# A 480-column matmul into two accumulators in the linear layers of a hybrid decoder step

## What is computed

```python
for layer in range(DEPTH):                       # DEPTH = 2
    xp, xs = rms_norm(hp, nw[0]), rms_norm(hs, nw[0])
    # layer 0: nsa(x @ w_in) @ w_out             w_in: 1024 x 2608, w_out: 1024 x 1024
    # layer 1: hgrn(x @ w_in) * gate @ w_out     w_in: 1024 x 4096, w_out: 1024 x 1024
    ...
    h = h + rms_norm(mixer_out, nw[1])
    a, g = split(rms_norm(h, nw[2]) @ w_gu)      # 1024 x 5632
    h = h + rms_norm((silu(a) * g) @ w_down, nw[3])   # 2816 x 1024
```

## Time and profile before

| | |
|---|---|
| time, three runs | 1673.37, 1675.85, 1679.09 us; median 1675.85 |
| profiled execution | span 1673.2 us from its first to its last instruction; no time of its own is listed beside it |
| PE busy | 1589.8 us, 95% of the span, 15534 matmuls and as many weight loads |
| DVE, ACT, POOL busy | 810.0, 554.3, 565.5 us |
| mean granted TensorE clock | 0.969 of full speed |
| largest groups | the six products of L1025, 6720 matmuls of 128x260 |

### The profile page before, as it was taken

The page is one execution under the profiler, slowest core; times in us unless marked ns, Lnnn a source line. Parts: engine busy times, 40 slices in busy tenths (PEclk is TensorE's granted clock), DMA queues, the critical chain, the costliest instruction groups (busy, mean ns, idle before and its releaser), DMA issues. The chain is left out here.

```text
span 1673.2 us, 38351 instructions
## 1 busy us (share of the span) xinstructions
PE 1589.8 (95%) x15534; PEld 1484.1 (89%) x15534; DVE 810.0 (48%) x1353; ACT 554.3 (33%) x1051; POOL 565.5 (34%) x505
## 2 busy tenths in 40 slices
PE   7997898999899999999998999999899999999996
PEld 7997885666599999999998899999799999999995
DVE  4331126566548344443148677675448343443145
ACT  4120115556455222222245433324255222222242
POOL 0002105677524534433016234332014443433013
PEclk9999888999999999999999999999899999999998
DMA  6855988877340222223343334333140222323342
GB/s 208 315 178 180 323 308 337 285 254 257 137 176 20 96 88 88 94 98 105 104 157 113 96 89 149 102 118 87 64 139 27 88 88 89 99 92 104 105 156 86
DMA packets 87375, 238.35 MB, mean 142 GB/s; under 512 B 18333, under 2 KB 21071, under 8 KB 85793
## 3 DMA queue, kind: packets, MB, share of 16 engines
q1 hardware_dynamic: 81528, 221.41, 39.1%
q0 software_dynamic: 3392, 11.02, 1.8%
q10 hardware_dynamic: 2314, 3.96, 0.7%
HBM read 217.81 MB, written 23.77 MB: 144 GB/s over the span
## 5 line engine op out<-in xcount | busy, mean ns | idle before, releaser
L867 DVE TENSOR_TENSOR layer_w_lo<-ring,layer_w_hi 128x1024 fp32r<-128x1024 f32 (+1 forms) x136 | 223.1, 1641 | 258.4 <-ACT layer_w_hi L746 258.4
L1025 PE MATMUL layer_ps<-layer_x_hi,layer_w_hi 128*128 128x260 f32 x1312 | 268.5, 284 | 3.8 <-DVE layer_w_lo L867 2.7
L1025 PE MATMUL layer_ps<-layer_x_hi,layer_w_lo 128*128 128x260 f32 x1312 | 267.8, 284 | 0.0
L1025 PE MATMUL layer_ps<-layer_x_lo,layer_w_hi 128*128 128x260 f32 x1312 | 267.3, 283 | 0.0
L746 ACT ACTIVATE layer_w_hi<-ring 128x1024 fp32r<-128x1024 f32 (+1 forms) x136 | 158.7, 1169 | 206.8 <-PE layer_ps L1025 206.8
L1025 PE MATMUL layer_ps<-layer_h_lo,layer_w_hi 128*128 128x260 f32 x960 | 218.0, 288 | 8.6 <-DVE layer_h_lo L876 8.6
L1025 PEld LDWEIGHTS layer_ps<-layer_x_hi,layer_w_hi 128*128 128x128 f32 x1312 | 204.2, 189 | 5.3 <-DVE layer_w_lo L867 2.9
L1025 PEld LDWEIGHTS layer_ps<-layer_x_hi,layer_w_lo 128*128 128x128 f32 x1312 | 204.1, 189 | 0.0
L1025 PEld LDWEIGHTS layer_ps<-layer_x_lo,layer_w_hi 128*128 128x128 f32 x1312 | 203.5, 189 | 0.1
L1025 PE MATMUL layer_ps<-layer_h_hi,layer_w_hi 128*128 128x260 f32 x704 | 172.8, 286 | 4.9 <-DVE layer_w_lo L867 4.9
L1025 PE MATMUL layer_ps<-layer_h_hi,layer_w_lo 128*128 128x260 f32 x704 | 170.2, 282 | 0.0
(11 more groups left out here) (334 smaller groups left out, 2954.7 us busy)
## 6 DMA issues: line engine op xcount, KB each, us to landing
ring<-in_w_gu SPq DMA_DIRECT2D x88, 512.0 KB, 3.2
ring<-in_w_down SPq DMA_DIRECT2D x48, 704.0 KB, 4.1
arena<-in_cache_cmp SPq DMA_DIRECT2D x68, 256.0 KB, 6.2
ring<-in_hgrn_w_in SPq DMA_DIRECT2D x32, 512.0 KB, 3.4
ring<-in_nsa_w_in SPq DMA_DIRECT2D x21, 512.0 KB, 4.5
kv_slot<-in_slc_kv SPq DMA_DIRECT2D x32, 256.0 KB, 4.5
arena<-in_slc_kv SPq DMA_DIRECT2D x32, 256.0 KB, 4.9
X<-in_slc_kv SPq DMA_DIRECT2D x32, 256.0 KB, 4.0
```

The costliest lines, as they stand in the source:

```text
L867: dve.tensor_tensor(self.w_lo[slot][:, 0:kcs * P], c.ring[:, s, 0:kcs * P], self.w_hi[slot][:, 0:kcs * P].bitcast(F32), ALU.subtract).then ...
L1025: mm = pe.matmul(bank[:, h, 0:TH], wt[slot][:, a], xt[:, x, COLS[h]], start=start and part == 0, stop=stop and part == 2)
```

## The change

The tokens are split into 280 first and 240 second columns (`FIRST`, `WIDE`), and the two banks of a unit are filled so that the 520 sums are contiguous: the first 280 end bank 0, the second 240 begin bank 1 (`tokens`, `part`). Bank 1 holds a second accumulator of 240 behind the first. For the second columns the products of the high weight with the high input and with the input's rest become one matmul of 2 x 240 = 480 columns, which reads both parts and writes both accumulators (`both_sums`); the parts of an operand now lie in one tensor for that. A chunk is five matmuls: 280, 480, 280, 280, 240. Behind a unit the two accumulators have to be added: a DVE `tensor_reduce` over two (`merge`).

In HGRN's input projection, `apart=False`, a chunk keeps six matmuls, of 280 and 240 columns, into one accumulator.

```diff
+FIRST = 280
+BANK_AT = 512 - FIRST
+WIDE = (FIRST, T - FIRST)
+def merge(dve, dst, banks):
+    return dve.tensor_reduce(dst, both_sums(banks).rearrange("p (two t) -> p t two", two=2), AX, ALU.add)
+
+def scaled_out(dve, dst, banks, rstd, merged, n):
+    merge(dve, dst[:, COLS[1]], banks).then_inc(merged, 1)
+    dve.tensor_tensor(dst[:, COLS[0]], part(banks, 0), rstd[:, COLS[0]], ALU.mult)
+    dve.wait_ge(merged, n)
+    return dve.tensor_tensor(dst[:, COLS[1]], dst[:, COLS[1]], rstd[:, COLS[1]], ALU.mult)
+
+def products(pe, banks, w_hi, w_lo, x, halves, start, stop, apart=True):
+    if 0 in halves:
+        pe.matmul(part(banks, 0), w_hi, x[:, 0, COLS[0]], start=start, stop=False)
+    if 1 in halves and not apart:
+        for x_part in range(2):
+            pe.matmul(part(banks, 1), w_hi, x[:, x_part, COLS[1]], start=start and x_part == 0, stop=False)
+    if 1 in halves and apart:
+        pe.matmul(both_sums(banks).rearrange("p (two t) -> p two t", two=2), w_hi, x[:, :, COLS[1]], start=start, stop=False)
+    if 0 in halves:
+        pe.matmul(part(banks, 0), w_hi, x[:, 1, COLS[0]], start=False, stop=False)
+    for h in halves:
+        mm = pe.matmul(part(banks, h), w_lo, x[:, 0, COLS[h]], start=False, stop=stop)
+    return mm
...
 def evac_nsa(c, HT):
-        eng.tensor_tensor(pairs((c.XW[:, n, :] if n < KC else HT[:, n - KC, :])), ps[j][:, :, 0:TH], pairs(c.rstd[:, :]),
-                          ALU.mult).then_inc(c.psum_free[j], 1)
+        scaled_out(eng, c.XW[:, n, :] if n < KC else HT[:, n - KC, :], ps[j], c.rstd, merged, n + 1).then_inc(c.psum_free[j], 1)
...
         def out(n, half=None):
-            act.activation(sq, src, ACT.Square).then_inc(mid.squared, 1)
-            act.activation(y, src, ACT.Copy).then_inc(self.half_out if first else c.psum_free[j], 1)
+            if half is None:
+                act.activation(Y[:, n, COLS[0]], part(ps[j], 0), ACT.Copy).then_inc(self.copied, 1)
+                act.wait_ge(self.copied, n + 1)
+            act.wait_ge(self.merged, n + 1)
+            act.sem_inc(c.psum_free[j], 1)
+            act.activation(sq, y, ACT.Square).then_inc(mid.squared, 1)
...
+        def second_out(n):
+            self.used(dve, n)
+            merge(dve, Y[:, n, COLS[1]], self.ps[n % RING]).then_inc(self.merged, 1)
+        def down_second_out(u, half):
+            self.down_used(dve, 2 * u + (9 if half else 1))
+            merge(dve, Y[:, u, COLS[1]], self.ps[u % RING]).then_inc(self.merged, 1)
...
         mid.post_mean(dve, own, 0)
+        second_out(4)
...
         for k in range(KC):
             mid.rest(dve, 0, k)
+            if k in (1, 4, 7):
+                second_out((k - 1) // 3 + 5)
...
+            if n in (2, 4, 6, 8):
+                down_second_out(n // 2 - 1, False)
...
+            if n in (18, 20, 22, 24):
+                down_second_out(n // 2 - 5, True)
```

More of the change, by code:

```diff
@@ L425, in token_sums @@
                 for h in range(2):
-                    mm = pe.matmul(bank[:, h, 0:TH], c.ones[:, :], squares[:, h * TH:(h + 1) * TH], start=start, stop=stop)
+                    mm = pe.matmul(part(bank, h), c.ones[:, :], squares[:, COLS[h]], start=start, stop=stop)
                 return mm
@@ L541, in sums @@
         pe.wait_ge(self.added, x + 1)
-        pe.matmul(self.bank[:, h, 0:TH], self.c.ones[:, :], self.ssq[:, COLS[h]], start=True, stop=True)\
+        pe.matmul(part(self.bank, h), self.c.ones[:, :], self.ssq[:, COLS[h]], start=True, stop=True)\
           .then_inc(self.summed, 1)
@@ L613, in gathered @@
         pe.wait_ge(self.inverse, 1)
-        pe.matmul(self.bank[:, 0, 0:TH], self.c.ones[:, :], self.ssq[:, COLS[0]], start=True, stop=True)\
+        pe.matmul(part(self.bank, 0), self.c.ones[:, :], self.ssq[:, COLS[0]], start=True, stop=True)\
           .then_inc(self.pre_summed, 1)
@@ L1047, in gate_up @@
                     pe.wait_ge(first.x_lo, halves[0] * KC + k + 1)
-                mm = products(bank, slot, self.xs, k, k, halves, k == 0, k == KC - 1)
+                mm = chunk(bank, slot, self.xs[:, :, k, :], k, halves, k == 0, k == KC - 1, first is not end)
                 if each is not None:
```

130 lines of the change are left out of this document (73 added, 57 removed).

## The result

The changed kernel takes 1691.65 us (median of four runs, 1686.75 to 1694.9) against 1674.61 for the kernel before (four runs, 1672.65 to 1679.09): a ratio of 1.009, 95% interval 1.0064 to 1.0117. It is slower by 17 us, where I had forecast 1647.4 us, 28 us faster. The profiled execution has a span of 1691.7 us and a time of 1693.49 us of its own. Two executions of the experiments, one of the kernel before and one with the split of 264 and 256, took some 2205 us at a granted clock of 0.65, and no ratio counts them.

What follows compares the result with a forecast made beforehand. PE's rate of starting 260-column matmuls was taken as the bound. Gains of 37.7 and 0.5 less losses of 0.8, 5.6, 2.5 and 0.8 gave 28.5 us less: 1647.4 us, range 1635 to 1669.

Steps and rivals of the forecast that it cites:

- a floor of this kind: Linear layers: a weight load sets a minimum of 120.1 ns between fp32r matmuls, hidden only under longer ones.
- 1072 chunks: Attention's input projection, mixer units, gate and up, first half of down: each chunk gains 35.2 ns, together 37.7 us.
- what I had named as proof against me: Signs of error: 480 columns over 210 ns, 240 under 115 or over 130, or PE waiting for DVE in gate and up.
- The squares: Plain f32 matmuls of 260 columns, read as 0.219 us apart, two clocks a column, with only 2.3 ns left over.
- The time follows the columns (slower): fp32r costs 0.462 ns a column at full clock, so chunks stay at 720.6 ns and merges cost 9.2 us: 1685, chance 0.06.
- Two other rivals: 11.8 ns on every matmul, 1672 us, chance 0.15; 240 fp32r columns at 400 ns, some 300 us lost, chance 0.05.
- Behind the mixers: Crossings behind each mixer, where DVE sets the end: merges and wider operations lose 2.8 us each, 5.6 us together.
- The chain merge, square, root: Crossing behind the mixer: ACT's square waits for the first merge and its root stands behind the square, 1.0 us.
- crossings cost double: Merges meet DVE and POOL slowing each other and 280 columns cost 123 ns: 31.3 us gained, 18 lost, 1662, chance 0.10.
- Second columns of down: Down's second columns: layer 0 loses 2.5 us to merges, layer 1 gains 0.5 us.
- First halves alone keep three matmuls a chunk, now of 280: nothing.: Chunks of first columns only: 3 x 121 ns instead of 360.3, so no gain.
- The 0.8 us at the end of attention's projection: End of attention's input projection: nothing covers DVE's longer evacuation, a loss of 0.8 us.

Runs made afterwards that it cites:

- the first experiment: Changed kernel with the 280/240 split kept but six matmuls a chunk everywhere and no merge: 1688.43 us, ratio 1.0051 to the kernel before.
- the third: Changed kernel with six matmuls a chunk and no merge in the mixers' output projections alone: 1694.01 us, ratio 1.0088 to the kernel before.
- the first two experiments: Changed kernel without wide matmul and merge everywhere (1688.43 us), then with them only in attention's input projection and gate and up (1683.44 us).

## Why the prediction was wrong

**The step that failed** is "I read the 120.1 ns as a floor of this kind, for fp32r weights, above the 108.3 + 2.3 = 110.6 ns that the columns need". The 120.1 ns were the columns: 260 at 0.46 ns. With the rest read as a floor I had 202.3 ns for 480 columns; it is 216.7 alone and 218.2 in the stream. I had 121 for 280; it is about 129. I had 120.1 for 240; it is about 110 in the stream and 113.1 alone. The chunk came to 714.7 instead of 685.4, and 1072 chunks at 6.6 ns would give 7 us in place of 37.7, an estimate from the measured gate and up units. The 480 over 210 and the 240 under 115 are what I had named as proof against me; for the 280 I had named nothing.

What misled me is the half clock. There 260 columns cost 216.9 ns, one cycle a column, and I concluded that a column at full clock costs half. At half clock fp32r takes one cycle a column; at full clock 480 columns take 8% more than 480 cycles (216.7 and 200.0 ns). The squares misled in the same way: they are plain f32, and a record of plain f32 has no such loss (402.5 at 480, two cycles a column). So neither of the two rows that I leaned on was fp32r at full clock; the only such row was the 120.1 itself, and it said 0.462 a column. Why fp32r streams slower is not shown: neither the load, nor one or two pieces (2.5 ns), nor the bank explains it.

**The rival that was right** is "The time follows the columns (slower)", at a chance of 0.06, 1685 us. Its 0.462 ns a column is close to what was measured, 0.45 to 0.46. It was 7 us low, and that nearness is partly luck: it had no gain and losses of 9.2 us, where the stages lost 21 to 24 us and gate and up gave back 4. Its deciding point, a gain under 8.6 ns a chunk, was met: 6.6.

Two other rivals fall with the widths: between 260 and 512 columns 2.6 ns and not 11.8 are left to each matmul, and 240 columns show no step (113.1 ns, not 400).

**The losses**, term by term:

- Behind the mixers I had 5.6 us; measured 10.4 to 11.5. The split alone gives 1.8 in the first experiment and 0.6 in the third, the merges some 9 to 11. The chain merge, square, root was as I said, and the wait for a rest grew from 0.66 to 3.7 us in sum, as I said (about 3). Missed were the second loop through ACT's queue and the half clock behind the waits, about 2.5 us of the two layers. So the rival "crossings cost double" (0.10) had the size of this term, and the gain beside it wrong.
- Second columns of down: I had -2.5 in layer 0 and +0.5 in layer 1. Together they lost 6 to 9 us. With six matmuls and no merge there they come to 101.4 us in the first two experiments and 103.0 in the one on down alone, against 102.5 before, so the merges and the wide matmul are the loss. In layer 1 the merges stand behind updates that are slow beside POOL's, which I had not seen.
- "First halves alone keep three matmuls a chunk, now of 280: nothing." The first part of down lost 3 us. By estimate, 88 such chunks a layer at 3 x 129 instead of 360.3 ns are 2.3 us, 4.7 in both layers, less 1.2 that the 176 full chunks beside them gain: 3.5.
- The merge itself: 0.64 us taken, 0.655 measured. In gate and up DVE stays hidden as I said: PE waits for nothing there. The 0.8 us at the end of attention's projection cannot be seen beside its 133.3 and 133.8.

The group of merges, DVE by shape (columns as in the earlier trace rows):

```profile
L130 DVE TENSOR_REDUCE mixer_out<-layer_ps 128x240 f32<-128x480 f32 x120 | 78.6, 655 | 243.2 <-PE layer_ps L153 241.7 <-ACT rstd L604 1.4
```

The account of the layers closes by steps of one edit: split alone +8.9, wide where covered -6.2, merges and wide matmul in down +6.4, in the mixers +11.0, together +20.1 of the +20.1 that the two profiles show. That it closes is by construction; that each step lies in the main in its own stage is what the stage sums show. Taking the merges out of down alone gives 4.0 to 7.2 us for the step of 6.4 (936.2 against 940.2 and 943.4).

## What to carry to other kernels

A floor and a price by the column give the same number at one width: before costing a change of width, find a second width of the same type at the same clock, or measure one, since a row at another clock or of another type prices that other thing. A small added operation costs nothing that shows on an engine with slack, and about twice its length in a queue where others wait (behind the mixers eight merges of 0.655 us cost 9 to 11 us), so follow what stands behind its waiter too (here merge, square, high part, rest, PE). Where a matmul pays by the column, cheaper columns (bf16 for the product that can bear it, grouped so that types change seldom) can gain what fewer matmuls do not: here 0.4%.

## What the runs showed of the hardware

- fp32r streams 7% slower than bf16 at full clock (216.7 and 202.6 ns for 480 columns). At half clock it takes one cycle a column (216.9 for 260).
- A plain f32 matmul leaves two records of some two cycles a column each (402.5 ns for 480 columns), 805 ns together.
- A matmul of 32 or 128 weight columns costs the same under 480 columns (216.8 and 216.7). The Trainium skill, "TensorE: Matmul & The Clock Gate", "Step-by-step: what each phase is for", says that loading the next weights takes no read bandwidth from the running matmul; these two series agree.
- Changing between fp32r and bf16 in every chunk cost the gain of the bf16 product: 230.11 us a layer mixed, 225.6 grouped.
- PE had idled 0.78, 1.59 and 0.19 us ahead of its starts at 512.40, 514.64 and 515.49; from 515.2 us the granted clock was 0.50, the 1.2 GHz level, for 10.2 us. With matmuls put into these waits it stayed at 2.4 GHz. Waits alone do not tell whether it falls: in the second columns of down of layer 0, PE waited 1.48, 1.03, 0.76 and 1.90 us with merges taken out of down and 1.49, 1.03, 0.77 and 1.89 with the split alone, and the clock fell, from 904.0 us, in the first alone.
